# A hybrid decoder trunk on one core: fourteen divisions of attention outputs move from VectorE to GpSimd

## The reference, cut to what matters

```python
def forget_attention(q, k, v, c_q, c_k, q_pos, k_pos):
    s = jnp.einsum('nqhd,nkhd->nhqk', q, k, preferred_element_type=jnp.float32) * (HEAD_DIM ** -0.5)
    s = s + (jnp.transpose(c_q, (0, 2, 1))[:, :, :, None] - jnp.transpose(c_k, (0, 2, 1))[:, :, None, :])
    causal = k_pos[None, :] <= q_pos[:, None]
    s = jnp.where(causal[None, None], s, NEG_INF)
    p = jax.nn.softmax(s, axis=-1)
    return jnp.einsum('nhqk,nkhd->nqhd', p.astype(v.dtype), v)
```

## Time and profile before

| what | value |
|---|---|
| time, median of 3 runs | 2518.68 us (2518.4 to 2519.05) |
| span of the profiled execution | 2517.1 us |
| PE busy | 2496.6 us, 99% |
| DVE busy | 1818.8 us, 72% |
| ACT busy | 1049.5 us, 42% |
| POOL busy | 24.1 us, 1% |
| attention on the prompt | about 1410 to 1667 us of the span |
| divisions (L1331) | 16, 19.7 us of DVE in all |

### The profile page before, as it was taken

The page is one execution under the profiler, slowest core; times in us unless marked ns, Lnnn a source line. Parts: engine busy times, 40 slices in busy tenths (PEclk is TensorE's granted clock), DMA queues, the critical chain, the costliest instruction groups (busy, mean ns, idle before and its releaser), DMA issues. The chain is left out here.

```text
span 2517.1 us, 45832 instructions
## 1 busy us (share of the span) xinstructions
PE 2496.6 (99%) x18268; PEld 2462.9 (98%) x18268; DVE 1818.8 (72%) x2467; ACT 1049.5 (42%) x1494; POOL 24.1 (1%) x48
## 2 busy tenths in 40 slices
PE   8999999999999999999999999999999999999999
PEld 8999999999999999999999999988999999999999
DVE  6434437766678998964445798988786666899987
ACT  4111124333343333355335787776653333333333
POOL 0000000000000000000000100010000000000000
PEclk9999999999999999999999999999999999999999
DMA  4111110333353313015424566645323333443112
GB/s 131 42 42 50 42 43 26 128 103 104 104 181 133 104 69 103 18 52 170 129 81 128 148 145 167 153 127 183 96 80 103 103 103 104 178 138 126 64 52 70
DMA packets 249037, 259.41 MB, mean 103 GB/s; under 512 B 18144, under 2 KB 184192, under 8 KB 248898
## 3 DMA queue, kind: packets, MB, share of 16 engines
q1 hardware_dynamic: 229510, 248.26, 31.8%
q10 hardware_dynamic: 19388, 9.20, 1.3%
HBM read 193.86 MB, written 63.42 MB: 102 GB/s over the span
## 5 line engine op out<-in xcount | busy, mean ns | idle before, releaser
L872 PE MATMUL ps<-h_op,w_op 128*128 128x268 f32 x4912 | 614.2, 286 | 0.2
L872 PEld LDWEIGHTS ps<-h_op,w_op 128*128 128x128 f32 x4912 | 609.6, 188 | 0.6 <-DVE w_op L912 0.6
L605 PE MATMUL ps<-x_hi,w_hi 128*128 128x358 f32 x1248 | 279.9, 330 | 2.0 <-DVE w_lo L589 1.7
L605 PE MATMUL ps<-x_hi,w_lo 128*128 128x358 f32 x1248 | 275.5, 327 | 0.0
L605 PE MATMUL ps<-x_lo,w_hi 128*128 128x358 f32 x1248 | 275.0, 326 | 0.0
L589 DVE TENSOR_TENSOR w_lo<-w_raw,w_hi 128x1024 fp32r<-128x1024 f32 x76 | 92.8, 1222 | 250.8 <-ACT w_hi L581 250.8
L883 ACT ACTIVATE w_op<-w_op_f 128x2048 fp32r<-128x2048 f32 (+1 forms) x54 | 97.6, 1808 | 381.6 <-PE ps L872 361.5
L605 PEld LDWEIGHTS ps<-x_hi,w_hi 128*128 128x128 f32 x1248 | 213.3, 189 | 5.0 <-DVE w_lo L589 2.2
L605 PEld LDWEIGHTS ps<-x_lo,w_hi 128*128 128x128 f32 x1248 | 215.8, 189 | 0.0
L605 PEld LDWEIGHTS ps<-x_hi,w_lo 128*128 128x128 f32 x1248 | 215.6, 189 | 0.0
L1069 DVE TENSOR_TENSOR t<-ps,t 128x536 f32<-128x536 f32 x180 | 128.7, 715 | 119.3 <-PE ps L817 110.4
(11 more groups left out here) (377 smaller groups left out, 5165.6 us busy)
## 6 DMA issues: line engine op xcount, KB each, us to landing
raw_a<-in_mlp_w SPq DMA_DIRECT2D x120, 256.0 KB, 3.1
h_op_f<-h_rows SPq DMA_DIRECT2D x24, 1072.0 KB, 6.6
w_op_f<-in_mlp_w SPq DMA_DIRECT2D x24, 1024.0 KB, 7.5
h_rows<-t SPq DMA_DIRECT2D x90, 268.0 KB, 2.1
w_raw<-in_conv_w_in SPq DMA_DIRECT2D x24, 512.0 KB, 3.8
w_raw<-in_w_kv SPq DMA_DIRECT2D x16, 512.0 KB, 4.8
w_raw<-in_w_o SPq DMA_DIRECT2D x16, 512.0 KB, 3.8
k_page<-in_cache_k SPq DMA_DIRECT2D x16, 512.0 KB, 4.6
```

The costliest lines, as they stand in the source:

```text
L605: mm = pe.matmul(PS[:, bank(s, g), 0:GW], w[:, s, k], x[:, k, g * GW:(g + 1) * GW], start=(at == 0 and n == 0), stop=(at == KC - 1 and n = ...
L872: mm = pe.matmul(PS[:, 2 * p + g, 0:QW], w[:, k, P * m:P * m + P], x[:, k, QW * g:QW * g + QW], start=(k == 0 and j == 0), stop=(k == tile ...
```

## The change

Divisions 0 to 13 are issued by GpSimd. Divisions 14 and 15 stay on VectorE. GpSimd does divisions 0 to 12 in a loop, each as soon as its `inv_sums` has landed and the division before it is done, behind the constants that it sets before head 0. Division 13 stands behind its constants in head 15. `divide` now also waits for the divisions before it.

```diff
-        def divide(h):
+        def divide(eng, h):
 
             m, hh = head(h)
             own, _ = halves(hh)
-            dve.wait_ge(inv_loaded[hh], 16 * (m + 1))
-            dve.tensor_tensor(QS[own, m, 0:NPR], OS[own, hh], INV[own, :], ALU.mult).then_inc(o_fin, 1)
+            eng.wait_ge(inv_loaded[hh], 16 * (m + 1))
+            ge(eng, o_fin, h)
+            eng.tensor_tensor(QS[own, m, 0:NPR], OS[own, hh], INV[own, :], ALU.mult).then_inc(o_fin, 1)
...
             extend(2)
-
-
+            for h in range(HEADS - 3):
+                divide(pool, h)
+            pool.wait_ge(o_fin, HEADS - 3)
             pool.wait_ge(v_lo, HEADS)
...
             pool.memset(CSLP[:, :].bitcast(F32), 0.0).then_inc(pad_zero, 1)
+            pool.wait_ge(pad_zero, 3)
+            divide(pool, HEADS - 3)
+            pool.wait_ge(o_fin, HEADS - 2)
             pool.wait_ge(d_mask, DB + 1)
...
                         reduce_max(h + 1, u)
-                        if h > 1 and u == 0:
-                            divide(h - 2)
...
-                if h == HEADS - 1 and g == 0:
-                    divide(h - 2)
...
             o_split_lo(6)
-            divide(HEADS - 2)
-            divide(HEADS - 1)
+            divide(dve, HEADS - 2)
+            divide(dve, HEADS - 1)
```

## The result

The changed kernel takes 2525.7 us (median of 8 runs, 2524.58 to 2529.05), the kernel before 2518.69 us (median of 8 runs beside it, 2517.84 to 2520.18). The ratio is 1.0029, with a 95% interval of 1.002 to 1.0038: slower by 7.0 us. The forecast was 2521.7 us, with a range of 2516.9 to 2527.0 that holds the result. What the prediction thought likeliest (0.68), a time within 0.2% of the one before, did not come. The profiled execution of the changed kernel is its longest run: its span is 2527.3 us, its time 2529.05 us.

The account below looks back on a forecast made before the run. PE, busy 2496.6 of 2517.1 us, was taken to bound the kernel. Stalls of 4.3 us less 1.3 credit gave +3.0: span 2520.1, median 1.6 above it, 2521.7 us; range 2516.9 to 2527.0.

Parts of the forecast that it names:

- For 8 and 12 ... I take half: Divisions 8 and 12, landing just before group 1's subtraction: half of GpSimd-first costs 0.95 and 0.98 us, 0.97 together.
- VectorE first (1, 2, 5, 6, 7, 9): In these divisions' heads group 1's subtraction starts before GpSimd's multiply: no stall, but nothing in hand.
- S: Start in each head of VectorE's low-probability subtraction of group 1; 1638.57 for division 12.
- its own formula: PE's stall at its use of group 1 when GpSimd starts first: landing + 3.27 us minus that use's time.
- division 10: Its inverse sums land so late that the multiply meets group 2's subtraction: 0.88 us of stall.
- rival 3: A slower GpSimd multiply, 2.8 us or more: +6 to +11 us, 2525 to 2530; chance 0.13.
- Both ties lost: Upper bound: a 2.8 us multiply and GpSimd first in divisions 8 and 12, +11.3 us with no credit.
- The credit: Time coming back in the five early heads from removing VectorE's divisions: −1.3 us.
- The multiply: GpSimd's 64x1040 multiply, taken as 2.3 us from selects' column price; bounds 1.1 and 2.8 us.
- Rival 1: GpSimd's multiply does not hold VectorE, or is short: −1.3 us, 2517.4; chance 0.23.
- Rival 2: The hold between GpSimd and VectorE lasts from start to end, whoever was first: +5.3 us, 2524.0; chance 0.17.
- Rival 4: VectorE, not PE, paces the steady head: 5.1 us comes back, −6.4 with the 1.3, 2512.3; chance 0.05.

Follow-up runs that it names:

- e8: The changed kernel, unaltered, run for a second profiled execution: one run, 2526.06 us.
- e2: The changed kernel with GpSimd's multiplies cut to the first of 1040 columns, same waits and semaphores: 2517.45 us against 2518.6 for the kernel before.
- e6: The changed kernel with GpSimd's divisions 0 to 12 behind the reduction preceding group 1's low-probability subtraction and a one-column memset: 2520.04 us against 2518.27.
- e1: The changed kernel with GpSimd waiting for group 1's low probabilities before each of divisions 0 to 12: 2522.89 us against 2518.6 for the kernel before.
- e3: The changed kernel with each GpSimd multiply replaced by a 64x1040 memset that reads nothing: 2518.16 us, ratio 0.9998.
- e4: The changed kernel with each GpSimd multiply replaced by a one-input 64x1040 copy: 2517.8 us, ratio 0.9999.
- e7: The changed kernel with each GpSimd division done twice into the same place, the second behind the first: one run, 2545.87 us.

## Why the prediction was right or wrong

**The step that failed** is the order. "For 8 and 12 ... I take half" and "VectorE first (1, 2, 5, 6, 7, 9)" assumed GpSimd first in five heads; it was first in 11. Divisions 1, 2, 5, 7 and 9, which the landings of one execution put 0.05 to 0.11 us behind S, came 0.06 to 0.52 us ahead of it, and 8 and 12 both stayed ahead. In undisturbed later heads S comes 3.9 us after the DMA's issue (division 12: 1647.16 − 1643.25 = 3.91; before, 1638.57 − 1634.66 = 3.91). The landing varies from 3.3 to 4.7 us. These are the landings of `inv_sums` in the kernel before, in the changed one and in e8:

```profile
DMA to landing us min/median/max: 3.5/3.9/4.7
...
DMA to landing us min/median/max: 3.4/3.8/4.3
...
DMA to landing us min/median/max: 3.3/3.5/4.4
```

The median is 3.5 us in the profiles of all ten experiments. So GpSimd is as a rule first by 0.4 us, and the one profile of the kernel before had late landings. Seven heads within 0.12 us of the edge were one bet, and it was taken from landings read to 0.1 us in one execution. The prediction named these landings as a weak step and yet priced them as if they were known. By its own formula a tie in a later head costs 3.27 − 2.18 = 1.09 us; with all seven ahead and without division 10 that gives, as an estimate, 4.3 − 0.88 + 0.97 + 5 · 1.09 = 9.8 us of stall, between the 8.3 of e8 and the 11.0 of the first profile.

**The range** held the result in part by luck. The forecast's own range (2519 to 2524) did not hold it. What carried the stated range up to 2527.0 was rival 3, a multiply of 2.8 us, and that did not come. "Both ties lost" was no bound either, since five more heads were as near to the edge.

**The size of each stall** was about right where the order was: 0.84 us were forecast for division 3, and its head grew by 1.04; 0.98 for division 12, if first, and its head grew by 1.07. The difference is 0.12 us of the multiply's length and 0.06 us more between the subtraction's end and PE's use; in division 12 the landing was 0.1 us earlier than before. The stalls add up to 8.3 us instead of 4.3.

**The credit** of −1.3 us came out as 2517.45 − 2518.6 = −1.15 us, though that ratio's interval holds 1. If it is real, it is in another place than I put it. The profiled spans differ by 1.3 us (2517.1 and 2515.8). The five early heads gave 0.34 us instead of 1.3; 1.16 us are the late values of one head (17.01 us before, 15.85 in e2). In the profile of the kernel before, ScalarE waits 1.8 us for these values; in none of the eleven others does it wait for them. There is one profile of the kernel before, so whether moving the division removed that wait or chance did stays open.

**Division 10**, 0.88 us, did not appear in the changed kernel. It is not the DMA that became so much faster (landing 4.3 us after the issue; before, 4.7): its issue had come late in the head, 2.94 us ahead of S, and now came 3.90 us ahead, as in the other heads. So the landing was late by 0.40 us and not 1.76, the subtraction of group 2 took 1.08 us, and the head is 15.97 us. That a late landing does cost what it holds of group 2 is seen in e6.

**"VectorE first: no stall"** was nearly right for a multiply that starts inside the subtraction (head 15.94 us, 0.14 more; e6 nearly the same) and 0.37 us short for one placed behind it (e1).

**The multiply** measured 2.417 us, 2.3 forecast, from a row of selects and the assumption on two reads. The prediction's bounds of 1.1 and 2.8 us hold it. The select's price, 0.19 us and 0.84 ns a column, fits the copy (1.05 us) and the one-column multiply (0.19 us); the multiply takes 2.14 ns a column, more than two turns of 0.84.

**The rivals.** Rival 1, no hold, is refuted by every long subtraction, and e3 shows what no hold looks like. Rival 2, a hold from start to end, was priced at +5.3 us and rested on the same wrong order, so that its time lies nearer to the result says nothing for it. (Two of its figures are off: half of both orders for 8 and 12 gives 1.4 and not 1.25 us, and the subtraction held to the end of the select would have taken 0.21 + 0.96 = 1.17 us, not 1.13.) The end of the hold decides against it: 0.13 us before the multiply's end in the changed kernel, 0.13 in e1, 0.14 in e4. The Trainium skill, "SBUF — State Buffer", section "Who interferes with whom", says that VectorE with two SBUF inputs contends with a GpSimd instruction that reads SBUF and not with one that only writes it, and that issue order decides. The traces agree: 2.12 us of hold behind the multiply, 0.59 behind the copy, none behind the memset, and 0.96 us for a subtraction that was first. The prediction's assumption that VectorE's reductions from PSUM are not held holds too: in e1 VectorE's masked maxima of 144 columns (from PSUM and one SBUF tile, 1642.56) lie inside the multiply and take 0.31 us, as in e2. The hold on the subtraction differs from the whole instruction by the 0.13 us of its record. Whether the reads end that much before the record does, or the hold before the reads, no run tells. Rival 3 did not occur; e7 shows it from the point at which the division ends behind ScalarE's copy. In the changed kernel the division ended 0.8 us or more ahead of that copy in every head of the loop. Rival 4 is refuted by e2: 13.21 us of VectorE in a head, and 15.80 us of head.

## What to carry to other kernels

Freeing an engine is worth only what waits for it; here 17 us of VectorE's work were worth at most about 1 us, which can hardly be told from nothing, and moving them cost 8 us elsewhere. Before an instruction with SBUF inputs goes to GpSimd, see which two-input VectorE instruction can start while it runs, and what that one has in hand: the price is the part of the hold beyond the slack. Where a DMA's landing decides the order, read it from more than one execution and price the heads near the edge for both outcomes, or take the landing out of it: place the GpSimd instruction by a semaphore behind the VectorE instruction, and cut it into parts that fit the gaps.

## What was not expected of the hardware

- The hold works in both directions and is shorter than the records: the waiting engine goes on 0.13 to 0.15 us before the recorded end of the other. Recorded durations contain the wait (0.96 becomes 3.22 us on VectorE, 2.42 becomes 2.75 on GpSimd), so an engine's busy time can grow when work is taken from it: VectorE 1818.8 to 1825.9 us.
- A lead of 0.01 us is enough for a whole hold: in the head of division 7 the multiply is recorded from 1563.66 and the subtraction from 1563.67, and that one took 3.22 us. With VectorE ahead by 0.11 us (division 2 in e8) the subtraction took 0.96 us and the multiply 3.12.
- GpSimd's multiply with two SBUF inputs follows its columns closely: 1, 208, 512, 528, 780, 832 and 1040 columns took 0.19, 0.63, 1.28, 1.33, 1.86, 1.97 and 2.42 us, some 2.14 ns for a column and 0.19 us fixed. A copy of 1040 took 1.05 us, a memset 0.96. Two inputs cost 2.3 times one at 1040 columns.
